# Sums of squares at the layer entries: wide VectorE additions for the second block, and modulation chunks, a value tile and DMAs at other places

## The chip, the core and the metric

The kernel runs on one core of a Trainium2 chip. The metric is the device time of one execution in microseconds, lower is better. Engines are named as in the profile: PE is TensorE, DVE is VectorE, ACT is ScalarE, POOL is GpSimd, SP is SyncE, which here issues the loads of the weights.

## The reference, cut to what matters

Two blocks run one after the other on x of 256 tokens by 1024 features, each with two layers. Block 1 is a mixer of two attentions and a convolutional feed-forward part, with norms that are scaled and shifted by a modulation `c @ mod_w`. Block 2 has five branches, one of them attention over a memory. Between the blocks stands the final norm of block 1.

```python
def _rmsnorm(x, g):
    xf = x.astype(jnp.float32)
    y = xf * lax.rsqrt(jnp.mean(xf * xf, axis=-1, keepdims=True) + EPS)
    return (y * g.astype(jnp.float32)).astype(x.dtype)

def first_block(...):
    for l in range(DEPTH):
        mod = c @ mod_w[l] + mod_b[l]
        sh1, sc1, g1, sh2, sc2, g2 = [m[:, None, :] for m in jnp.split(mod, 6, axis=-1)]
        h = _rmsnorm(x, norm1_g[l]) * (1.0 + sc1) + sh1
        x = x + g1 * _mixer(h, positions, w_in[l], ...)
        h = _rmsnorm(x, norm2_g[l]) * (1.0 + sc2) + sh2
        x = x + g2 * _conv_ffn(h, w_up[l], conv_w[l], conv_b[l], w_down[l])
    return _rmsnorm(x, final_g)

def second_block(x, mem, norm_pre, norm_post, ...):
    for l in range(DEPTH):
        h = rmsnorm(x, norm_pre[l])
        (...) = split_cols(h @ w_in[l])
        ...
        mem_kv = rmsnorm(mem, mem_norm[l]) @ w_mem_kv[l]
        ...
        x = x + rmsnorm(merged @ w_out[l], norm_post[l])
    return x
```

## The kernel before

**Layout.** Features lie on the partitions: x is eight tiles (KD = 8) of 128 features by 256 tokens. A weight matrix comes from memory in chunks of 1 MB, each of two blocks of 128x1024, into a ring of five buffers (`ring`). To keep float32 accuracy at PE's faster rate each block is split into a rounded part `w_hi` (ACT, L1649) and the rest `w_lo` (DVE, L2042); the input is split likewise into `h_hi` and `h_lo`, and PE does three matmuls for a product (L1351, L1352, L1357; L1389, L1390, L1395 for tiles with tokens on the partitions). Six split blocks are held (SPLIT), so a new block's `w_hi` must wait until PE has read the block six before it.

**The plan.** `plan()` writes one list of steps, and each engine goes through it and does its own part of each step. The order of the list is thus the order on every engine. Ahead of its part of a step ACT splits blocks up to `st.upto`, DVE up to `st.behind`, both set by which blocks PE has used so far (`st.first`). In the last two tiles of a row of statistics and at a root of block 2 the splits of DVE stand at other places than elsewhere (the end of DVE's loop).

**A norm.** Eight steps `stat` make the squares of x on ACT (L1683) into `h_val`. The step `root` sums them over the features by matmuls with ones into `sums`: either POOL has added tiles 0 to 4 and PE sums five tiles' sum and tiles 5 to 7 (L1413, L1416 three times), or, where x comes as a row of its own (`in_row`: the first norm in block 2's layers, with x just written by the final norm or by the sum of the branches), PE sums all eight (L1416 eight times). ACT then does Ln and Exp (L1688, L1690), DVE a Newton step (L2150 to L2156), and the step `norm` makes `h_val` on DVE (L2182), `h_hi` on ACT (L1746 with a shift, L1748 without), `h_lo` on DVE. PE's next tiles need h.

**What PE does while a norm is made.** In block 1 chunks of the modulation (step `mod`, eight matmuls of 32x256, L1435) fill the gap: `gap_mod` puts one ahead of the norm and one behind it, if the last row of four chunks has been taken up; `some_mod` puts the others between other tiles, 46 in all. In block 2 it is the keys and values of the memory, which need no h of x: at the first entry (layer 0, at 880 us) one tile of keys and two token tiles of values (`mv`), then the root; at the second entry (layer 1, at 1205 us) two tiles of keys, then the root, then the two token tiles of values.

**The SP queue** (L1304 to L1314) issues the loads of all 266 chunks in the order of their use, each when its ring buffer is free, and at the end stores x in two parts of four tiles.

Of the kernel before, what the change touches and what calls it, by code (L numbers as in the profile page):

```python
# [84 lines left out]
class Step:  # L85
# [8 lines left out]
    def __init__(self, kind, subs, first, l=None, t=None, j=None, i=None, k=None, n=None, v=None, W=None,  # L94
# [5 lines left out]
                 last_ready=None, group=None, early=None):  # L100
# [8 lines left out]
        self.gate, self.sc_taken, self.last_ready, self.group, self.early = gate, sc_taken, last_ready, group, early  # L109
# [70 lines left out]
def plan():  # L180
# [9 lines left out]
    state = dict(parts=[], summed=None, loaded=None, added={}, all_by_pe={})  # L190
# [84 lines left out]
    def stats(after, src, tiles=None):  # L275


        i = p.count("norm")
        in_row = bool(after) and isinstance(after[0], tuple)
        state["all_by_pe"][i] = in_row  # L280
        state["added"][i] = n = p.counts.get("added", 0) if in_row else p.count("added")
        for k in range(KD + 1):
            if tiles and k < KD:
                after.append(tiles(k))
            if k:
                p.add("stat", k=k - 1, i=i, n=None if in_row else n, atts=p.counts.get("att", 0), src=src, hn=p.counts.get("h_norm", 0),
                      after=after[k - 1] if after else None)
        return i

    def root(i, mode):  # L290

        p.add("root", i=i, n=None if state["all_by_pe"][i] else state["added"][i], atts=p.counts.get("att", 0), mode=mode)

    def gap_mod():
        if queue and not state["summed"]:
            mod(*queue.pop(0))

    def norm(kind, after, src, i=None, rooted=False, mods=False, **more):

        if i is None:  # L300
            i = stats(after, src)
        if not rooted:
            root(i, kind)
        if mods:
            gap_mod()
        hn = p.count("h_norm") if kind in ("mod", "gain", "mem") else None
        p.add("norm", mode=kind, i=i, hn=hn, src=src, **more)
        if mods:
            gap_mod()
# [32 lines left out]
    for l in range(L1):  # L342
# [151 lines left out]
        def down(j):  # L494

            if j < len(early):
                return early[j]
            ps = fm("dn", dn[j], j=j, l=l).ps
            some_mod()
            return ps  # L500
        x_stats = stats([], "x", down)
        reduce_mod()
    plan2(p, fm, plain, norm, stats, att, att_out, att_turn, x_stats)
# [5 lines left out]
def plan2(p, fm, plain, norm, stats, att, att_out, att_turn, x_stats):  # L509
# [20 lines left out]
    kv_taken[0] += token_tiles(v0, 2, what="mv", l=0, src="mem")  # L530
    p.add("load_bias", l=0, after=None)
    norm("gain", None, "x", first, l=0)
# [427 lines left out]
def program(nc, weights, small, const, levels, buckets, far, x_t, mem_t, pos, scratch, mod_rows, mem_root, out):  # L960
    p = schedule()
    ctx = ExitStack()
    with ctx:
# [147 lines left out]
        sums_ready = sem("sums_ready")  # L1111
        mean_ready = sem("mean_ready")
# [181 lines left out]
        def _(sp):  # L1294
# [18 lines left out]
            sp.wait_ge(stored, 16 * KD // 4)  # L1313
# [3 lines left out]
        def _(pe):  # L1317
# [86 lines left out]
            def root(st):  # L1404
# [622 lines left out]
        def _(ve):  # L2027
# [130 lines left out]

            def vals(st):
# [501 lines left out]
            do = dict(setup_tables=setup_tables, setup=setup, bias=bias, vals=vals, mod=mod, modred=modred, modsum=modsum, root=root, norm=norm, mem_again=mem_again,  # L2661
# [92 lines left out]
```

## Time and profile before

| | |
|---|---|
| Median of 3 runs | 1542.07 us (1542.05 to 1544.58) |
| Profiled execution: its own time | 1542.8 us |
| Profiled execution: span, first to last instruction | 1541.0 us |
| PE, PEld busy | 1496.3 us (97%), 1433.5 us (93%) |
| DVE, ACT, POOL busy | 1143.7 (74%), 833.4 (54%), 31.4 us (2%) |
| Mean granted clock of PE | 0.993 |
| Loads of the ring | 266 of 1,024 KB |

How to read it: busy time is that of the engine's own instructions; PE and PEld (its weight loads) overlap, and the ends of pipelined matmuls are modelled, so a matmul that is shown as 0.28 us long may begin 0.12 us after the one ahead. In the timelines the number in brackets is the time for which the engine stood idle ahead of the row, and what ended it. A count beside a matmul that stands alone in its row can hold its weight load too (eight matmuls and eight loads are "x16"). PEclk is the granted clock, 1.00 for 2.4 GHz and 0.50 for 1.2 GHz. "First entry" is block 2's layer 0, at 875 to 900 us, "second entry" its layer 1, at 1203 to 1226 us.

### The profile page before, as it was taken

The page shows a single profiled execution, that of the slowest core. Times are in us where ns is not written, and L with a number is a line of the kernel's source. Part 1 is how long each engine was busy: PE and PEld are TensorE (multiplying, and loading weights), DVE is VectorE, ACT ScalarE, POOL GpSimd, SP SyncE. Part 2 cuts the span into 40 slices and gives each one's busy share as a digit, 9 for nine tenths or more (in the row PEclk, how much of TensorE's full clock was granted, in tenths as well). Part 3 has the DMA queues.
Part 4 walks back from the last instruction along what each step waited for, and adds up shares of the span by engine and source line. Part 5 has one row for each costly group of instructions (what it writes and reads, how often), then busy time and mean ns, then how long its engine had stood idle before and what let it go on. Part 6 is the DMA issues. An engine that isn't in the chain of part 4 may idle for free.

```text
span 1541.0 us, 31309 instructions
## 1 busy us (share of the span) xinstructions
PE 1496.3 (97%) x12608; PEld 1433.5 (93%) x12608; DVE 1143.7 (74%) x2202; ACT 833.4 (54%) x1509; POOL 31.4 (2%) x36
## 2 busy tenths in 40 slices
PE   6999999999999999999999999999999999999997
PEld 4898898999998999989999989999999999999997
DVE  5758566888646586769996678878966988888774
ACT  3655545655435646446555655645555754645453
POOL 0000001000000000010001000000000000000000
PEclk9999999999999999999999999999999999999998
DMA  9654555676776452454545543443446444444430
GB/s 393 251 216 184 202 223 192 219 275 247 275 272 252 168 214 87 157 196 165 179 179 194 219 164 113 169 185 138 154 152 246 150 154 163 167 163 141 169 129 28
DMA packets 47840, 290.51 MB, mean 189 GB/s; under 512 B 9992, under 2 KB 12296, under 8 KB 13136
## 3 DMA queue, kind: packets, MB, share of 16 engines
q1 hardware_dynamic: 38880, 280.83, 49.0%
q10 hardware_dynamic: 8816, 7.67, 1.5%
q8 instruction: 101, 1.65, 0.4%
q14 instruction: 43, 0.35, 0.1%
HBM read 286.09 MB, written 2.39 MB: 187 GB/s over the span
## 4 chain that ended last, share of the span: by engine, by line
PE 57%; DVE 1%; ACT 1%; DMA 0%; issue 0%; DVEq 0%; ACTq 0%
PE bank L1351 17%; PE bank L1357 16%; PE bank L1352 16%; PE bank L1601 2%; PE sums L1526 1%; PE sums L1416 1%; PE bank L1390 1%; PE bank L1395 1%; PE bank L1389 1%; PE bank L1508 1%; PE bank L1499 1%; DMA mem_x<-mem_t 0%; DVE w_lo L2042 0%; ACT w_hi L1649 0%; PE bank L1533 0%
## 5 line engine op out<-in xcount | busy, mean ns | idle before, releaser
L1351 PE MATMUL bank<-h_hi,w_hi 128*128 128x256 f32 x2256 | 632.8, 288 | 8.9 <-ACT h_hi L1746 3.7
L1352 PE MATMUL bank<-h_hi,w_lo 128*128 128x256 f32 x2256 | 622.3, 283 | 0.0
L2042 DVE TENSOR_TENSOR w_lo<-ring,w_hi 128x1024 fp32r<-128x1024 f32 x436 | 523.4, 1222 | 106.4 <-ACT w_hi L1649 103.8
L1357 PE MATMUL bank<-h_lo,w_hi 128*128 128x256 f32 x2256 | 575.9, 283 | 0.0
L1649 ACT ACTIVATE w_hi<-ring 128x1024 fp32r<-128x1024 f32 x436 | 449.2, 1054 | 131.4 <-PE bank L1357 130.9
L1351 PEld LDWEIGHTS bank<-h_hi,w_hi 128*128 128x128 f32 x2256 | 432.8, 192 | 22.9 <-issue 17.9
L1352 PEld LDWEIGHTS bank<-h_hi,w_lo 128*128 128x128 f32 x2256 | 433.0, 192 | 0.6 <-issue 0.5
L1357 PEld LDWEIGHTS bank<-h_lo,w_hi 128*128 128x128 f32 x2256 | 405.2, 192 | 0.0
L1351 PE MATMUL bank<-a_hi,w_hi 128*128 128x256 f32 x352 | 99.6, 283 | 1.0 <-DVE w_lo L2042 0.7
L1352 PE MATMUL bank<-a_hi,w_lo 128*128 128x256 f32 x352 | 98.3, 279 | 0.0
L1357 PE MATMUL bank<-a_lo,w_hi 128*128 128x256 f32 x352 | 98.2, 279 | 0.0
L1389 PE MATMUL bank<-w_hi,h_hi 128*128 128x256 f32 (+1 forms) x304 | 86.6, 289 | 3.9 <-ACT h_hi L1746 2.9
L1390 PE MATMUL bank<-w_lo,h_hi 128*128 128x256 f32 (+1 forms) x304 | 85.7, 286 | 0.0
L1883 ACT ACTIVATE conv_a<-bank,sm 128x256 f32<-128x256 f32 x44 | 24.8, 564 | 105.2 <-PE bank L1357 105.2
L1395 PE MATMUL bank<-w_hi,h_lo 128*128 128x256 f32 (+1 forms) x304 | 81.7, 287 | 0.0
L1351 PE MATMUL bank<-y_hi,w_hi 128*128 128x256 f32 x288 | 79.3, 280 | 0.0
L1352 PE MATMUL bank<-y_hi,w_lo 128*128 128x256 f32 x288 | 78.8, 278 | 0.0
L1357 PE MATMUL bank<-y_lo,w_hi 128*128 128x256 f32 x288 | 75.7, 281 | 0.0
L1944 ACT ACTIVATE sig<-bank 128x256 f32<-128x256 f32 x80 | 30.3, 379 | 78.1 <-PE bank L1357 77.5
L1351 PEld LDWEIGHTS bank<-a_hi,w_hi 128*128 128x128 f32 x352 | 66.1, 188 | 4.7 <-issue 3.3
L1389 PEld LDWEIGHTS bank<-w_hi,h_hi 128*128 128x128 f32 x304 | 59.6, 196 | 7.2 <-issue 5.9
L1352 PEld LDWEIGHTS bank<-a_hi,w_lo 128*128 128x128 f32 x352 | 66.2, 188 | 0.0
(336 smaller groups left out, 2345.7 us busy)
## 6 DMA issues: line engine op xcount, KB each, us to landing
ring<-weights SPq DMA_DIRECT2D x266, 1024.0 KB, 4.9
pos_bias<-scratch ACTq DMA_DIRECT2D x4, 512.0 KB, 5.6
x<-x_t ACTq DMA_DIRECT2D x1, 1024.0 KB, 6.9
scratch<-line ACTq DMA_DIRECT2D x1, 1024.0 KB, 5.6
mem_x<-mem_t ACTq DMA_DIRECT2D x1, 1024.0 KB, 6.7
mem_second<-mem_t ACTq DMA_DIRECT2D x1, 1024.0 KB, 6.2
out_t<-x SPq DMA_DIRECT2D x2, 512.0 KB, 2.6
co<-const SPq DMA_DIRECT2D x1, 462.0 KB, 7.2
```

Source lines behind the costliest of these rows:

```text
L1351: pe.matmul(to, WH[:, b % SPLIT, o, :], hi[:, k, :], start=(i == 0), stop=False)
L1352: pe.matmul(to, WL[:, b % SPLIT, o, :], hi[:, k, :], start=False, stop=False)
L1357: last = pe.matmul(to, WH[:, b % SPLIT, o, :], lo[:, k, :], start=False, stop=(i == n - 1))
L1389: pe.matmul(o, q, WH[:, s:s + m.n, k, :], start=(k == 0), stop=False)
L1390: pe.matmul(o, q, WL[:, s:s + m.n, k, :], start=False, stop=False)
L1395: last = pe.matmul(o, q, WH[:, s:s + m.n, k, :], start=False, stop=(k == KD - 1))
L1416: m = pe.matmul(sums[:, 0:S], ones, hb[:, k, :], start=(st.n is None and k == 0), stop=(k == KD - 1))
L1601: m = pe.matmul(to[:, (2 * g + s) * P:(2 * g + s + 1) * P], k[half, g, s * P:s * P + P], q[half, g, t * P:t * P + P], start=True, stop=True)
L1649: act.activation(WH[:, b % SPLIT], ring_half(b), ACT.Copy).then_inc(w_hi, 1)
L1883: act.activation(to[:, st.j % 3, :], bank[u.bank][:, 0:S], ACT.Identity, scale=ss(("conv_w", st.l, 2), c), bias=ss(("conv_b", st.l), c)).t ...
L1944: act.activation(sig2[:, st.j % 4, :], bank[st.ps.bank][:, 0:S], ACT.Tanh, scale=0.5).then_inc(taken[st.ps.bank], 1)
L2042: ve.tensor_tensor(WL[:, b % SPLIT], ring_half(b), WH[:, b % SPLIT].bitcast(F32), ALU.subtract).then_inc(w_lo_v, 1)
```

## The change

Six edits are made together.

1. In the two norms that PE summed alone, DVE adds the squares: tiles 2, 3 onto 0, 1 once tile 3 is squared; tiles 6, 7 onto 4, 5 once tile 7 is; then these onto the first two. Each is one addition of 128x512. PE sums the two tiles that are left.
2. `norm` calls `gap_mod` twice ahead of the norm.
3. Behind the last tile of the down projection no chunk of the modulation stands any more.
4. At the first entry the root stands between the two token tiles of values.
5. SP waits for the chunk (0, 0, 3), the last of the first two rows of the modulation, to land before it issues the next load.
6. x is stored in four parts of two tiles.

```diff
@@ stats, root
+        row = p.count("added_row") if in_row else None
+        state["row"][i] = row
...
@@ norm
         if mods:
+            gap_mod()
             gap_mod()
@@ down
             ps = fm("dn", dn[j], j=j, l=l).ps
-            some_mod()
+            if j < KD - 1:
+                some_mod()
@@ plan2
-    kv_taken[0] += token_tiles(v0, 2, what="mv", l=0, src="mem")
+    values = token_tiles(v0, 2, what="mv", l=0, src="mem")
+    kv_taken[0].append(next(values))
     p.add("load_bias", l=0, after=None)
-    norm("gain", None, "x", first, l=0)
+    root(first, "gain")
+    kv_taken[0] += values
+    norm("gain", None, "x", first, rooted=True, l=0)
@@ block.sync
                 sp.dma_start(ring[c % RING][:], weights[c]).then_inc(loaded[c % RING], 16)
-            for k in range(0, KD, 4):
-                sp.wait_ge(x_z, (L2 - 1) * KD + k + 4)
-                sp.dma_start(out[:, k:k + 4], x[:, k:k + 4]).then_inc(stored, 16)
+                if kind == "mod" and what == (0, 0, 3):
+                    wait_loaded(sp, c)
+            for k in range(0, KD, 2):
+                sp.wait_ge(x_z, (L2 - 1) * KD + k + 2)
+                sp.dma_start(out[:, k:k + 2], x[:, k:k + 2]).then_inc(stored, 16)
...
@@ root of the tensor engine
-                for k in range(0 if st.n is None else ADDED + 1, KD):
-                    pe.wait_ge(sq_done, KD * st.i + k + 1)
-                    m = pe.matmul(sums[:, 0:S], ones, hb[:, k, :], start=(st.n is None and k == 0), stop=(k == KD - 1))
+                if st.row is not None:
+                    pe.wait_ge(row_sum, 3 * st.row + 3)
+                for k in range(2) if st.row is not None else range(ADDED + 1, KD):
+                    if st.row is None:
+                        pe.wait_ge(sq_done, KD * st.i + k + 1)
+                    m = pe.matmul(sums[:, 0:S], ones, hb[:, k, :], start=(st.n is None and k == 0),
+                                  stop=(k == (KD - 1 if st.row is None else 1)))
@@ vector engine
+            def stat(st):
+
+                if st.row is None or st.k not in (3, KD - 1):
+                    return
+                ve.wait_ge(sq_done, st.i * KD + st.k + 1)
+                a = st.k - 3
+                tt(hb[:, a:a + 2, :], hb[:, a:a + 2, :], hb[:, a + 2:a + 4, :], ALU.add).then_inc(row_sum, 1)
+                if a:
+                    ve.wait_ge(row_sum, 3 * st.row + 2)
+                    tt(hb[:, 0:2, :], hb[:, 0:2, :], hb[:, 4:6, :], ALU.add).then_inc(row_sum, 1)
```

DVE at the second entry, before: from the last sums of x (macc holds the normed sum of the branches) to the Newton step on `sums`.

```order
L2047 TENSOR_TENSOR macc_121<-macc_121,rsq 128x256
L2047 TENSOR_TENSOR x<-x,macc_121 128x256 x3
L2042 TENSOR_TENSOR w_lo<-ring4,w_hi 128x1024 x2
L2150 TENSOR_SCALAR mean2<-sums 128x256
L2047 TENSOR_TENSOR rsq<-guess 128x256
```

And now. `h_val_50<-h_val_50 128x512` is a wide addition of squares; the second and third wait for the last square and for each other.

```order
L2061 TENSOR_TENSOR macc_121<-macc_121,rsq 128x256
L2061 TENSOR_TENSOR x<-x,macc_121 128x256 x3
L2056 TENSOR_TENSOR w_lo<-ring4,w_hi 128x1024
L2061 TENSOR_TENSOR h_val_50<-h_val_50 128x512
L2056 TENSOR_TENSOR w_lo<-ring4,w_hi 128x1024
L2061 TENSOR_TENSOR h_val_50<-h_val_50 128x512 x2
L2164 TENSOR_SCALAR mean2<-sums 128x256
L2061 TENSOR_TENSOR rsq<-guess 128x256
```

The two splits stand where they stood, one on either side of the first addition, and the other two additions behind both. On PE the root's matmuls, now two, stand at their old place, between the keys and the values.

ACT at the first entry, before: the squares, the copies of the memory's keys and values (`mk_t`, `m_v`), the splits, the root and h.

```order
L1683 ACTIVATE h_val_50<-x 128x256 x8
L1914 ACTIVATE mk_t_96<-bank4 128x256
L1649 ACTIVATE w_hi<-ring1 128x1024
L1760 ACTIVATE m_v_97<-bank5 128x256
L1760 ACTIVATE m_v_97<-bank6 128x256
L1649 ACTIVATE w_hi<-ring2 128x1024 x2
L1907 DMA pos_bias_105<-scratch 128x4x256 x2
L1688 ACTIVATE guess<-sums,co 128x256
L1690 ACTIVATE guess<-guess 128x256
L1748 ACTIVATE h_hi<-h_val_50 128x256 x8
```

And now (lines are 14 further down in this function).

```order
L1697 ACTIVATE h_val_50<-x 128x256 x8
L1928 ACTIVATE mk_t_96<-bank4 128x256
L1663 ACTIVATE w_hi<-ring1 128x1024
L1774 ACTIVATE m_v_97<-bank5 128x256
L1921 DMA pos_bias_105<-scratch 128x4x256 x2
L1702 ACTIVATE guess<-sums,co 128x256
L1704 ACTIVATE guess<-guess 128x256
L1774 ACTIVATE m_v_97<-bank6 128x256
L1663 ACTIVATE w_hi<-ring2 128x1024 x2
L1762 ACTIVATE h_hi<-h_val_50 128x256 x8
```

The copy of the second value tile and two splits moved from ahead of the root to between the root and h.

The modulation's chunks on PE move by one place in the gaps of block 1: at 251 us three stand behind the sums (two before), at 465 us three behind them (one ahead and two behind before), at 676 us one (two before). Their number, 46, is the same.

## Rows read from the trace of the kernel before

**Rows 1.** Who waited for whom, of PE: total us, times, longest us.
```profile
PE bank L1351 <- ACT h_hi L1746: 3.7, 2, 1.9
PE bank L1351 <- ACT h_hi L1748: 3.6, 1, 3.6
PE bank L1389 <- ACT h_hi L1746: 2.9, 2, 2.0
```

**Rows 2.** Timeline of PE, first entry: start us, us, engine, line, tiles, count [idle].
```profile
884.22 0.28 PE L1389 MATMUL bank<-w_hi,h_hi 128*128 128x256 f32 x1
887.10 3.62 PE L1416 MATMUL sums<-h_val,co 128*128 128x256 f32 x16
894.35 0.36 PE L1351 MATMUL bank<-h_hi,w_hi 128*128 128x256 f32 x1 [3.63 <-ACT h_hi L1748]
```

**Rows 3.** Busy us by stretch: from:to, length, PE, PEld, DVE, ACT, POOL, PEclk, DMA.
```profile
680.00:684.00 4.00, 3.57 (x30) 3.60 (x31) 3.82 (x11) 2.60 (x6) 0.00 (x0) 1.00 1.01 428
895.00:898.00 3.00, 3.00 (x16) 3.00 (x15) 3.00 (x9) 1.74 (x5) 0.00 (x0) 0.50 0.03 5
474.00:478.00 4.00, 3.95 (x22) 3.98 (x23) 4.00 (x11) 2.35 (x5) 0.00 (x0) 0.64 1.02 428
```

**Rows 4.** Timeline of PE, second entry.
```profile
1210.71 4.28 PE L1416 MATMUL sums<-h_val,co 128*128 128x256 f32 x16
1214.63 0.47 PE L1389 MATMUL bank<-w_hi,mem_second_hi 128*128 128x256 f32 x1
```

**Rows 5.** Timeline of ACT, second entry.
```profile
1212.95 1.09 ACT L1683 ACTIVATE h_val<-x 128x256 f32<-128x256 f32 x3 [0.25 <-DVE x L2047]
1216.37 0.48 ACT L1688 ACTIVATE guess<-sums,co 128x256 f32<-128x256 f32 x1
```

**Rows 6.** Timeline of DVE, second entry.
```profile
1212.50 1.09 DVE L2047 TENSOR_TENSOR x<-x,macc 128x256 f32<-128x256 f32 x3
1213.51 2.36 DVE L2042 TENSOR_TENSOR w_lo<-ring,w_hi 128x1024 fp32r<-128x1024 f32 x2
```

**Rows 7.** Timeline of DVE: additions of 128x512 elsewhere.
```profile
1010.01 1.28 DVE L2047 TENSOR_TENSOR hg_exp<-hg_cum 128x512 f32<-128x512 f32 x2
```

**Rows 8.** Timeline of DVE, first entry.
```profile
884.26 1.21 DVE L2042 TENSOR_TENSOR w_lo<-ring,w_hi 128x1024 fp32r<-128x1024 f32 x1
```

**Rows 9.** Timeline of ACT, first entry.
```profile
887.30 0.38 ACT L1760 ACTIVATE m_v<-bank 128x256 f32<-128x256 f32 x1 [1.02 <-PE bank L1395]
888.53 1.05 ACT L1649 ACTIVATE w_hi<-ring 128x1024 fp32r<-128x1024 f32 x1
893.68 0.81 ACT L1748 ACTIVATE h_hi<-h_val 128x256 fp32r<-128x256 f32 x2 [2.00 <-DVE h_val L2182]
```

**Rows 10.** Timeline of PE, two gaps of block 1.
```profile
251.22 1.93 PE L1435 MATMUL bank<-ring,c_wide 128*32 128x256 f32 x32
...
676.64 1.93 PE L1435 MATMUL bank<-ring,c_wide 128*32 128x256 f32 x32
```

**Rows 11.** Timeline of DVE, gap at 465 us.
```profile
465.83 4.62 DVE L2042 TENSOR_TENSOR w_lo<-ring,w_hi 128x1024 fp32r<-128x1024 f32 x4
```

**Rows 12.** Line L1309, window 468 to 469: ring loads issued, and their landing.
```profile
L1309 SPq DMA_DIRECT2D ring<-weights x1: 328/328/328, 468.3 to 468.3; - x1
DMA to landing us min/median/max: 4.6/4.6/4.6
```

**Rows 13.** Line L1309, window 22 to 27.
```profile
L1309 SPq DMA_DIRECT2D ring<-weights x2: 327/328/328, 23.2 to 26.2; - x2
DMA to landing us min/median/max: 7.6/7.7/7.9
```

**Rows 14.** Timeline of PE and ACT, the start.
```profile
30.91 1.56 PE L1435 MATMUL bank<-ring,c_wide 128*32 128x256 f32 x16 [0.95 <-DMA ring<-weights]
37.78 3.89 ACT L1649 ACTIVATE w_hi<-ring 128x1024 fp32r<-128x1024 f32 x4
```

**Rows 15.** DMA issues: out<-in, queue, count, KB each, us to landing.
```profile
out_t<-x SPq DMA_DIRECT2D x2, 512.0 KB, 2.6
```

More of the change, by code:

```diff
@@ L99, in __init__ @@
                  lag=None, dir=None, prevn=None, k0=None, k1=None, ys=None, gate=None, sc_taken=None,
-                 last_ready=None, group=None, early=None):
+                 last_ready=None, group=None, early=None, row=None):
         self.kind, self.subs, self.first, self.upto, self.behind = kind, subs, first, None, None
@@ L108, in __init__ @@
         self.scale, self.lag, self.dir, self.prevn, self.k0, self.k1, self.ys = scale, lag, dir, prevn, k0, k1, ys
-        self.gate, self.sc_taken, self.last_ready, self.group, self.early = gate, sc_taken, last_ready, group, early
+        self.gate, self.sc_taken, self.last_ready, self.group, self.early, self.row = gate, sc_taken, last_ready, group, early, row
 class Plan:
@@ L188, in plain @@
         return p.matrix([tile_cols(name, lead, [(c0 + P * j, P)], rows) for j in range(n)])
-    state = dict(parts=[], summed=None, loaded=None, added={}, all_by_pe={})
+    state = dict(parts=[], summed=None, loaded=None, added={}, all_by_pe={}, row={})
     def mod(l, g, part):
@@ L285, in stats @@
             if k:
-                p.add("stat", k=k - 1, i=i, n=None if in_row else n, atts=p.counts.get("att", 0), src=src, hn=p.counts.get("h_norm", 0),
+                p.add("stat", k=k - 1, i=i, n=None if in_row else n, row=row, atts=p.counts.get("att", 0), src=src, hn=p.counts.get("h_norm", 0),
                       after=after[k - 1] if after else None)
@@ L290, in root @@
     def root(i, mode):
-        p.add("root", i=i, n=None if state["all_by_pe"][i] else state["added"][i], atts=p.counts.get("att", 0), mode=mode)
+        p.add("root", i=i, n=None if state["all_by_pe"][i] else state["added"][i], row=state["row"][i], atts=p.counts.get("att", 0), mode=mode)
     def gap_mod():
@@ L502, in plan, with plan2 @@
         reduce_mod()
-    plan2(p, fm, plain, norm, stats, att, att_out, att_turn, x_stats)
+    plan2(p, fm, plain, norm, root, stats, att, att_out, att_turn, x_stats)
     return p
-def plan2(p, fm, plain, norm, stats, att, att_out, att_turn, x_stats):
+def plan2(p, fm, plain, norm, root, stats, att, att_out, att_turn, x_stats):
     order = ("sc", "at", "mem", "cf", "hg")
@@ L1111, in program @@
         sums_ready = sem("sums_ready")
+        row_sum = sem("squares_of_a_row_added")
         mean_ready = sem("mean_ready")
@@ L1309, in _ @@
                 sp.dma_start(ring[c % RING][:], weights[c]).then_inc(loaded[c % RING], 16)
-            for k in range(0, KD, 4):
-                sp.wait_ge(x_z, (L2 - 1) * KD + k + 4)
-                sp.dma_start(out[:, k:k + 4], x[:, k:k + 4]).then_inc(stored, 16)
-            sp.wait_ge(stored, 16 * KD // 4)
+                if kind == "mod" and what == (0, 0, 3):
[3 more added lines that the diff above has]
+                sp.dma_start(out[:, k:k + 2], x[:, k:k + 2]).then_inc(stored, 16)
+            sp.wait_ge(stored, 16 * KD // 2)
         @block.tensor
@@ L2659, in m2end @@
                 m2_low(st.l, KD - 1)
-            do = dict(setup_tables=setup_tables, setup=setup, bias=bias, vals=vals, mod=mod, modred=modred, modsum=modsum, root=root, norm=norm, mem_again=mem_again,
+            do = dict(setup_tables=setup_tables, setup=setup, bias=bias, vals=vals, mod=mod, modred=modred, modsum=modsum, stat=stat, root=root, norm=norm, mem_again=mem_again,
                       rope=rope, decay=decay,
```

## Prediction

> **What bounds the kernel now.** I read the page first, then who waited for PE, then the timelines of the places that the change touches, then the granted clock by stretch. The page's first part shows PE busy for 97% of the span: what shortens PE's own row of work, or a wait of PE, shortens the run, and little else does. PE's waits are few and sit at the layer entries, where a sum of squares must pass through ACT and DVE before the next input h exists [rows 1]: 3.7 us for two gaps of block 1 that end on L1351 (at 255 and 680 us), 2.0 of the 2.9 for the gap at 474 us, 3.6 us at the first entry of block 2. There PE ends its work at 884.22 plus one token tile, 887.10, sums eight tiles of squares until 890.72, and then stands until 894.35 [rows 2]. That wait has a second price. After it the granted clock of 895 to 898 us is 0.50, the 1.2 GHz level, with 16 matmuls in 3 us, where 24 took 2.88 us from 884.22 to 887.10; it is 1.00, the 2.4 GHz level, from 680 to 684 us, after a wait of 1.9 us, and 0.64 from 474 to 478 us, after a shorter wait and one of 2.0 us with short chunks between [rows 3]. Three us at the lower level cost 1.5 us of PE.
>
> At the second entry of block 2, 1210 us, PE has no such wait: its eight sums begin at 1210.71, each as its square comes, and the value tiles begin at 1214.63 [rows 4]. The last three squares end at 1214.04, and ACT, busy with other work, takes the sum up only at 1216.37 [rows 5].
>
> **The second entry, PE's loss.** This is the largest term. PE's row now stands at one wait for three wide additions, with two sums behind it and 48 matmuls of the value tiles behind these. The additions stand on DVE among the splits of weights (w_lo). In the rows of before, x is finished at 1213.59, and two splits run from 1213.51 to 1215.87, so 1.18 us each, back to back with no wait [rows 6]. A wide addition of 128x512 is 0.69 us long, and two of them begin 0.59 to 0.6 apart (1.28 less 0.69) [rows 7]. In the new order: split until 1214.69; first addition (its squares are long done) until 1215.3; second split until 1216.5; second addition until 1217.1; the third waits for it, 0.1, and ends at 1217.8, 3.8 us after the last square. PE then does two sums. At the price of the first entry's eight, 3.62 / 8 = 0.45 us [rows 2], they end at 1218.7. Before, the value tiles began at 1214.63, so PE loses 4.1 us. ACT's Ln moves from 1216.37 to 1218.8, h is ready in time for the tile behind the value tiles, and nothing gives the loss back: PE has no wait behind it that could shrink.
>
> The same wait lasts from 1210.71 to 1217.8, 7.1 us, twice the one of 3.6 us that was followed by the lower clock. I take 4 us at 0.50 after it, 2.0 us of loss, between 0 (the clock spared) and 3.5 us (7 us of it, as long as at the first entry and again as much, as the wait is twice as long). Sum of this entry: 6.1 us, from 4.1 to 7.6. In case the splits did not stand in the way, the additions would end at 1214.1 + 0.6 + 0.1 + 0.6 = 1215.4 and the sums at 1216.3, which is 1.7 us instead of 4.1.
>
> The Trainium skill (TensorE: Matmul & The Clock Gate, section on how the gate's oscillation bites in real kernels) says that waits between groups of matmuls let the gate fall back to half rate, so that each group behind a wait starts slow. By it the 7.1 us are certain to cost clock, and both of the new waits at the first entry are suspect; the rows agree for 3.6 us and show that 1.9 us went free [rows 1 and 3].
>
> **The first entry.** Here the root now stands behind the first of two value tiles, so PE reaches it at 884.22. DVE ends x at 884.34 and would start its split at 884.26 [rows 8]; now the first addition comes first, until 884.9, the split until 886.1, then two additions, until 887.4. PE waits 3.2 us, sums two tiles until 888.4 (2.3 us sooner than 890.72), and does the second value tile, 2.88 us, until 891.3. The chain through ACT and DVE would give h at 888.4 + 3.63 = 892.0. But on ACT the copy of that second value tile and two splits (w_hi) now stand ahead of h_hi, and these splits overwrite the blocks that this tile reads. Before, from the end of this tile, 887.10, to the end of the splits, 889.58, is 2.5 us, and from the start of h_hi to PE's resumption 0.67 [rows 2 and 9]. So h_hi starts at 891.3 + 2.5 = 893.8 and PE resumes at 894.4 or 894.5, against 894.35: the 2.3 us are taken by the copy and splits, net 0.1, which I count as nothing. One wait of 3.6 us has become two, of 3.2 and of 3.1, around 3.8 us of work. If the clock falls in the first, the second value tile runs at half rate, up to 2.9 us more, and the next group as before: bounds are 1.6 us below nothing (no fall at all: 3.2 us at 0.50 are no longer there) and 4 us. I take 1.5, near the half of a tile, because 3.2 us is nearer to the wait that cost clock than to the one that did not. DVE's own two later splits move behind its norm as well; the blocks that they fill are read only after three more tiles, some 9 us, so I count 0 (2.4 us, two splits, if that cover failed).
>
> **The gaps of block 1.** A chunk of the modulation is 0.96 us of PE (two are 1.93 [rows 10]). The number of chunks is unchanged; what counts is how many stand in a wait. At 251 us there are three instead of two and the wait of 1.9 shrinks to 0.9: a gain of 0.96. At 465 us the one that stood ahead of the sums now stands behind them, so three as before. At 676 us there is one instead of two, since the other was used up earlier, and the wait grows to 2.8: a loss of 0.96 in the place where this chunk now runs. Net 0. Two things hang on it. At 465 us the third chunk needs a ring buffer that is free only when the second of four splits ends, 465.83 + 2.3 = 468.15 [rows 11]; a load issued at 468.3 there landed 4.6 us later, 472.9 [rows 12]. PE would have done two chunks by 471.3, waits until 472.9, and ends the third at 473.9, just ahead of h at 474.05: 0, up to 1 us. And DVE does four splits until 470.45 there and sums the modulation behind them before it looks at the root, so sums of squares that end sooner bring nothing. At 676 us a wait of 2.8 us may now bring the lower clock; 3.2 us of it cost 1.6. I take half, 0.8. That the fall at 474 us vanishes is the other bound, 1.5 us below nothing; its waits keep their lengths, so I take 0.
>
> **The start.** The queue now holds back the loads behind the last chunk of the first row. The loads issued at 23.2 and 26.2 us took 7.6 and 7.9 us [rows 13]: the first landed at 30.8, the second at 34.1, so one did not come at the expense of the other, the first was not slowed by more than the chunks ahead of it, and holding the second back speeds nothing. PE's wait for it is 0.95 us [rows 14], which bounds the gain. The later loads start up to 4.7 us later; the first is split by ACT at 37.78 [rows 14], and with 4.6 us to landing it comes at 35.5, 2.3 us ahead. I take 0, from 0.95 of gain to 1 of loss.
>
> **The end.** The store of 512 KB took 2.6 us to land [rows 15]. The last one is now 256 KB. At the rate of the load of 1,024 KB in 4.6 us [rows 12], the bound above is 256 / 1024 of 4.6, 1.2 us, the bound below nothing; I take 0.6.
>
> **The sum.** 6.1 + 1.5 + 0 + 0.8 + 0 - 0.6 = 7.8 us longer. The profiled execution took 1542.8 us with a span of 1541.0; its sum would be 1550.6. The median of the runs is 1542.07, and the forecast against it 1549.9 us, 0.5% slower.
>
> **The rivals.** First, the clock is spared (ends as no change): the two shorter waits of the first entry leave it at full (-1.6), so does the gap that ends at 474 us (-1.5), and the second entry pays only its 4.1, with the end's -0.6: +0.4, 1542.5 us. It is one mechanism, the clock's answer to a wait, and it decides from the wait of 7.1 us at 1210 us on. For it speaks that 1.9 us went free; against it, that 3.6 did not. Chance 0.12, for anything at or near this. Second, the clock answers worse: 4 at the first entry, 7.6 at the second, 1.6 at 676 us, 1 at 465, less 0.6: +13.6, 1555.7 us. For it speaks that the first entry has two waits in place of one; chance 0.13. Third, the wide additions are not held by the splits at the second entry, because DVE reaches them sooner than the rows of before allow: 1.7, with 1.5 of clock for a wait of 4.7 us, and the other terms as above (1.5 + 0.8 - 0.6): +4.9, 1547.0 us; against it stands the order, where one split is written between them; chance 0.15. My forecast has 0.55. The 0.05 left are for a real gain, for which no mechanism here adds up to 3 us.
>
> **From this to the numbers.** Faster or slower by over 0.2%, 3.1 us, is what a measurement of this kernel can tell from no change. Faster 0.05; same 0.15 (the first rival, a little of the third); slower 0.80. The range reaches from 1544.5, between the first and third rivals, to 1555.0, just short of the second.
>
> **What would show it.** At the second entry PE stands idle for some 7 us ahead of two sums, released by DVE's additions, with two w_lo ahead of them; a clock of 0.50 follows. At the first entry PE resumes with h within 0.5 us of the time after x that it has now, behind w_hi and not behind DVE. The gap at 676 us shows 2.8 us of wait. Wrong it would be if the second entry's sums are released under 2 us after the last square, or if the clock stays at 1.00 there.

## The result, and the profile after

The changed kernel took 1552.36 us (median of 4 runs, 1551.5 to 1553.35) against 1542.06 us for the kernel before in the same session (4 runs, 1541.78 to 1544.58): a ratio of 1.0060, 95% interval 1.0048 to 1.0072. It is 0.6% slower. The forecast was 1549.9 us, with a range from 1544.5 to 1555.0 and a chance of 0.80 for slower. The profiled execution took 1551.5 us, with a span of 1549.7.

PE's waits in the changed kernel, in the columns of [rows 1]:

```profile
PE bank L1449 <- DMA ring<-weights: 18.5, 4, 10.6
PE sums L1429 <- DVE h_val L2061: 10.2, 2, 7.0
PE bank L1361 <- ACT h_hi L1760: 3.7, 2, 2.7
PE bank L1361 <- ACT h_hi L1762: 2.9, 1, 2.9
```

The second row is new: PE waits for DVE's additions, 3.2 us at the first entry and 7.0 at the second. The wait for h_hi at the first entry has shrunk from 3.6 to 2.9 us, the one at 680 us has grown from 1.9 to 2.7.

**The second entry.** The timelines of PE, DVE and ACT answer to [rows 4 to 6]:

```profile
1220.72 2.05 PE L1429 MATMUL sums<-h_val,co 128*128 128x256 f32 x4 [7.01 <-DVE h_val L2061]
1222.20 0.78 PE L1399 MATMUL bank<-w_hi,mem_second_hi 128*128 128x256 f32 x1
...
1216.28 1.22 DVE L2056 TENSOR_TENSOR w_lo<-ring,w_hi 128x1024 fp32r<-128x1024 f32 x1
1217.42 0.69 DVE L2061 TENSOR_TENSOR h_val<-h_val 128x512 f32<-128x512 f32 x1
1218.02 1.22 DVE L2056 TENSOR_TENSOR w_lo<-ring,w_hi 128x1024 fp32r<-128x1024 f32 x1
1219.15 1.42 DVE L2061 TENSOR_TENSOR h_val<-h_val 128x512 f32<-128x512 f32 x2
...
1215.73 1.09 ACT L1697 ACTIVATE h_val<-x 128x256 f32<-128x256 f32 x3 [0.25 <-DVE x L2061]
```

The squares are done at 1216.82; DVE has two splits among its additions and ends them at 1220.57, 3.75 us later. PE's two sums then take 1.5 us in place of 0.9, because the clock has fallen; the value tiles begin at 1222.20, 16.1 us behind the mark at 1206.13 (the start of the root's matmuls on `mean`, shown below), where before they began 11.3 us behind it. Of these 4.8 us the lower clock inside the sums makes 0.6.

**The first entry** answers to [rows 2, 8 and 9]:

```profile
888.88 1.10 PE L1429 MATMUL sums<-h_val,co 128*128 128x256 f32 x4 [3.17 <-DVE h_val L2061]
897.21 0.55 PE L1361 MATMUL bank<-h_hi,w_hi 128*128 128x256 f32 x1 [2.87 <-ACT h_hi L1762]
...
892.42 0.88 DVE L2207 SCALAR_TENSOR_TENSOR h_val<-x,sm,rsq 128x256 f32<-128x256 f32 x2
...
894.38 0.38 ACT L1774 ACTIVATE m_v<-bank 128x256 f32<-128x256 f32 x1 [3.44 <-PE bank L1405]
894.66 1.99 ACT L1663 ACTIVATE w_hi<-ring 128x1024 fp32r<-128x1024 f32 x2
896.55 0.71 ACT L1762 ACTIVATE h_hi<-h_val 128x256 fp32r<-128x256 f32 x2
```

DVE has the first two tiles of h_val at 893.3, but ACT takes them up only at 896.55, behind the copy of the second value tile and two splits.

**The clock**, to be held against [rows 3]: from:to, length, PE busy, PEclk, DMA share, GB/s.

```profile
474.00:478.00 4.00, 3.08 (x33) 1.00 1.00 424
682.00:686.00 4.00, 4.00 (x24) 0.62 0.63 260
889.00:893.00 4.00, 4.00 (x20) 0.61 0.46 157
1219.00:1223.00 4.00, 2.28 (x7) 0.50 0.63 221
```

The fall at 474 us is gone; one at 682 us, one at 889, and the one around 1219 us are new. The last begins inside the wait: from 1216 us on the rows add up to 3.4 us of clock not granted, of which 1.8 fall behind the wait's end at 1220.72, where they cost PE something.

**Where the 8.7 us of span came from.** The root's matmuls on POOL's sum (L1413, now L1423) mark eight points of PE's row. The distances between them show each place by itself. The last two, of before and of after:

```profile
1203.34 0.59 PE L1413 MATMUL sums<-mean,co 128*128 128x256 f32 x2
1528.14 0.59 PE L1413 MATMUL sums<-mean,co 128*128 128x256 f32 x2
```

```profile
1206.13 0.59 PE L1423 MATMUL sums<-mean,co 128*128 128x256 f32 x2
1536.48 0.59 PE L1423 MATMUL sums<-mean,co 128*128 128x256 f32 x2
```

The same for every profile of this study (us; each column is the distance between two such starts, the last one that from the last start to the end of the span):

| kernel | start, to 249 | gaps of block 1, 249 to 834 | 834 to 877 | first entry, 877 to 1203 | second entry, 1203 to 1528 | end |
|---|---|---|---|---|---|---|
| before | 248.91 | 584.72 | 43.11 | 326.60 | 324.80 | 12.86 |
| store_alone | 249.07 | 583.78 | 43.47 | 326.57 | 324.79 | 12.82 |
| hold_alone | 248.26 | 583.96 | 43.10 | 327.48 | 324.78 | 12.82 |
| mods_alone | 249.69 | 585.45 | 43.11 | 326.60 | 324.78 | 12.87 |
| first_adds_alone | 248.60 | 584.01 | 43.12 | 326.55 | 324.78 | 12.84 |
| first_adds_moved | 252.93 | 584.08 | 43.10 | 328.23 | 324.79 | 12.87 |
| second_adds_alone | 251.76 | 584.55 | 43.47 | 326.57 | 330.66 | 12.79 |
| second_between | 250.62 | 583.61 | 43.11 | 327.60 | 326.26 | 12.80 |
| h_before_splits | 249.20 | 584.32 | 43.10 | 322.28 | 324.81 | 12.79 |
| gaps_filled | 248.43 | 582.40 | 43.11 | 323.81 | 324.78 | 12.87 |
| after | 250.38 | 584.22 | 43.47 | 328.06 | 330.35 | 13.22 |
| filled_wait | 249.26 | 584.09 | 43.10 | 328.21 | 328.56 | 13.18 |
| splits_later | 250.02 | 584.52 | 43.47 | 325.66 | 328.37 | 13.26 |

How to read it: where eight kernels do the same thing at the second entry they agree within 0.03 us, so a difference there is the edit's. The start differs by over 4 us among kernels that do the same, and the first entry by 1.1 us, so single profiles say less there. After less before is 1.47 - 0.50 + 0.36 + 1.46 + 5.55 + 0.36 = 8.70 us. The 0.36 from 834 to 877 us is no part of the change: 43.47 stands in four of the thirteen profiles, with the edits and without them (store_alone, second_adds_alone), and 43.1 in the others.

### The profile page after: what moved, and what is told of

The parts are those of the page before. It is cut to its first block, busy times and chain, and to the rows that moved or that the text cites. A ratio compares the mean times of both kernels' runs of the same rounds, so it can differ in the third digit from the quotient of the medians.

```text
span 1549.7 us, 31270 instructions
## 1 busy us (share of the span) xinstructions
PE 1492.4 (96%) x12584; PEld 1432.0 (92%) x12584; DVE 1148.8 (74%) x2208; ACT 833.9 (54%) x1509; POOL 31.3 (2%) x36
## 4 chain that ended last, share of the span: by engine, by line
PE 56%; DVE 3%; ACT 2%; issue 0%; DVEq 0%; ACTq 0%
PE bank L1361 16%; PE bank L1367 16%; PE bank L1362 16%; PE bank L1615 2%; PE sums L1540 1%; PE bank L1400 1%; PE bank L1399 1%; PE bank L1405 1%; ACT w_hi L1663 1%; DVE w_lo L2056 1%; PE bank L1522 1%; PE bank L1513 1%; PE sums L1429 0%; DVE macc L2061 0%; DVE x L2061 0%
## 5 line engine op out<-in xcount | busy, mean ns | idle before, releaser
L1449 PE MATMUL bank<-ring,c_wide 128*32 128x256 f32 x736 | 51.0, 401 | 18.5 <-DMA ring<-weights 18.5
```

The source lines that it names most:

```text
L1449: m = pe.matmul(to[q:q + 32, 0:256], cpad[:, k, :], w[:, k, :], start=(k < 4), stop=(k >= 4), tile_position=(0, q))
```

## The experiments

Each kernel was timed against runs of the kernel before on the same chip; these had medians of 1543.65, 1543.52 and 1543.33 us in the three sessions and scattered from 1539.8 to 1548.5, more than in the first one. So the ratios are the measure, and the table above shows where.

### The parts alone

**hold_alone**: before, and

```diff
                 sp.dma_start(ring[c % RING][:], weights[c]).then_inc(loaded[c % RING], 16)
+                if kind == "mod" and what == (0, 0, 3):
+                    wait_loaded(sp, c)
```

> The kernel before with one part of the change alone: the queue of loads waits for the last chunk of the first modulation row. By the prediction this costs nothing (0.95 us of gain to 1 us of loss): 1542.1 us. By a reading of the two profiles the held queue is what delays that chunk: in the changed kernel it is issued at 22.8 us and lands 8.9 us later, where before it took 7.6 to 7.9, PE waits 4.4 us for it and stands 1.5 us behind at 40 us. Then this kernel takes 1543.6 us, PE's wait ends near 31.7 us, and all the lag is there by 40 us. If the lag came from something else in the changed kernel, PE's first h is at 35.2 us as before.

Measured: ratio 1.0003 (0.9993 to 1.0012). PE's wait for the chunk and its first h, in this kernel:

```profile
30.36 1.07 PE L1445 MATMUL bank<-ring,c_wide 128*32 128x256 f32 x16 [0.64 <-DMA ring<-weights]
34.30 0.36 PE L1395 MATMUL bank<-w_hi,h_hi 128*128 128x256 f32 x1 [1.71 <-ACT h_hi L1756]
```

and in first_adds_moved, which holds nothing back at the start:

```profile
31.71 1.93 PE L1445 MATMUL bank<-ring,c_wide 128*32 128x256 f32 x16 [4.53 <-DMA ring<-weights]
```

My reading of the two profiles had been wrong: the late chunk is chance. From issue to landing it takes 7.5 or 7.6 us in nine of the thirteen profiles and 8.9 or 9.0 in four, two of these with the hold (after, splits_later) and two without (first_adds_moved, second_between). PE's first h comes between 34.3 and 36.5 us; the four with the hold have 34.30, 35.41, 36.32 and 36.45, the nine without it 34.76 to 36.39. The forecast value, 0, stands.

**mods_alone**: before, and

```diff
         if mods:
+            gap_mod()
             gap_mod()
...
-            some_mod()
+            if j < KD - 1:
+                some_mod()
```

> The kernel before with the moved modulation chunks alone: a second one in the gap before each norm of block 1, none behind the last down tile. The prediction had 0.8 us of loss (the wait of 2.8 us at 676 us brings the lower clock, 465 us is neutral): 1542.9 us. By the two profiles: 1.0 gained ahead of the sums at 465 us, 1.4 lost to the third chunk's load behind them, 1.5 gained since the clock does not fall at 474 us, 1.5 lost since it falls at 681 us, 0.7 to 0.9 gained at a wait for w_lo at 827 us if that wait vanishes. That is 0.5 us of gain at most: 1541.6 to 1542.3 us.

Measured: ratio 1.0009 (1.0000 to 1.0018), 0 to 2.8 us slower. PE at the gaps at 465 and 676 us, and the clock:

```profile
474.03 1.07 PE L1445 MATMUL bank<-ring,c_wide 128*32 128x256 f32 x16 [0.20 <-DMA ring<-weights]
681.44 0.55 PE L1357 MATMUL bank<-h_hi,w_hi 128*128 128x256 f32 x1 [2.72 <-ACT h_hi L1756]
```

```profile
682.00:686.00 4.00, 4.00 (x25) 0.66 0.73 307
```

The fall at 682 us stands in all four profiles with a wait of 2.7 us there, and in none of the eight with 1.9. It costs 1.5 us: from h to PE's next wait, for w_lo at 700 us, PE takes 19.1 us in all eight and 20.5 to 20.6 in the four. Earlier falls are another matter (below): over the whole stretch from 249 to 834 us the four kernels with the moved chunks have a mean of 584.57 us, the eight with the old ones 584.13, a loss of 0.4 us with a scatter as large. The forecast was 0.8. It is that small because three of the four have no other fall in this stretch, while each of the eight has one. In mods_alone, which has falls at 468 and 550 us besides, the third chunk at 465 us waits only 0.20 us for its load because the lower clock has made PE late (its two chunks ahead take 3.0 us in place of 1.9); in the other three it waits 1.8 to 2.0.

**first_adds_moved**: before, with edits 1 and 4 at the first entry only (`row` is counted only where `after[0][0] == "xn"`).

> The kernel before with the first entry of block 2 as changed (three wide additions, the root between the two value tiles), and nothing else. By the prediction: 0.1 us of logic, since h_hi on ACT stands behind the copy of the second value tile and two splits, and 1.4 of clock: +1.5 us, 1543.6 us, with a wait of 3.2 us ahead of the sums and one of about 3 behind the second value tile. By the rival in which the clock is spared it is 1.6 us of gain, 1540.5 us. The changed kernel's profile has PE's lag grow by 1.3 us there.

Measured: ratio 1.0007 (0.9995 to 1.0018). In the profile the first entry takes 328.23 us, 1.6 more than before's 326.60, and the changed kernel and filled_wait have 328.06 and 328.21. Both waits are there (3.2 and 2.9 us in its profile), and the clock falls behind both. The first fall slows the second value tile, so that h comes 19.1 us behind the mark, here and in the changed kernel (897.21 less 878.07), against 17.6 before. The clock:

```profile
892.00:896.00 4.00, 4.00 (x24) 0.57 0.14 46
899.00:903.00 4.00, 3.75 (x19) 0.57 0.02 4
```

The run's median shows 0.2 us, its interval reaches to 2.8, so the 1.5 us rest on the profiles: three with this code at 328.1 to 328.2, and seven with the code of before at the entry or with first_adds_alone's at 326.6 to 327.6.

**second_adds_alone**: before, with edit 1 at the second entry only.

> The kernel before with the three wide additions at block 2's second entry alone. By the prediction (two splits of weights stand among the additions, PE waits 7.1 us, then runs 4 us at the 1.2 GHz level) +6.1 us: 1548.2 us. By the rival in which the splits do not hold the additions it is 3.2 us: 1545.3 us. In the changed kernel's profile PE's lag grows by 5.6 us there; if that is the additions' own doing, the same must show here without the other parts: 1547.7 us.

Measured: ratio 1.0049 (1.0034 to 1.0064), 5.2 to 9.9 us; 1549.82 against 1543.65 us. The stage takes 330.66 us, 5.9 more than before. PE's wait and the clock:

```profile
PE sums L1423 <- DVE h_val L2055: 7.1, 1, 7.1
```

```profile
1218.00:1222.00 4.00, 1.07 (x3) 0.57 0.37 90
```

This one edit makes most of the result by itself, at the size forecast (6.1), and not at that of the third rival (3.2). The five ratios of the parts alone (the fifth, store_alone, follows) add up to 1.0064, against 1.0060 for all parts together, each known to 0.001 or 0.0015: no effect of the parts on each other is needed.

**store_alone**: before, with the four stores.

> The kernel before with its output stored in four pieces of 256 KB in place of two of 512 KB, and nothing else. The prediction had 0.6 us of gain (the last store lands sooner). In the profiles of the changed kernel and of two runs built on it, the time from the last value of x to the end is 3.1 us as before, and between mean and rsq on DVE 0.4 us of idle time stand that before has not. If the stores bring nothing and those 0.4 us come with another part, this kernel takes 1542.1 us and the last root to the end 12.8 us; if they come with the stores, 13.2 us.

Measured: ratio 0.9996 (0.9986 to 1.0005), end 12.82 us. The stores bring nothing: the 0.6 us of my sum were not there. I had scaled the time to landing with the size, and it hardly depends on it: 2.6 us for 512 KB [rows 15], and in this kernel

```profile
out_t<-x SPq DMA_DIRECT2D x4, 256.0 KB, 2.5
```

The 0.4 us of idle time on DVE that stand in the changed kernel's end come with none of the parts tried alone; they are in all three kernels that have all parts, and what makes them stays open (the rows are the changed kernel's).

```profile
1538.91 0.42 DVE L2164 TENSOR_SCALAR mean<-sums 128x256 f32<-128x256 f32 x1 [11.97 <-ACT guess L1702]
1539.78 0.43 DVE L2061 TENSOR_TENSOR rsq<-guess 128x256 f32<-128x256 f32 x1 [0.45 <-DVE mean L2164]
```

### What the second entry's loss is made of

**filled_wait**: the changed kernel, and ahead of PE's wait for the additions

```diff
+                for _ in range(14 if st.row == 1 else 0):
+                    pe.matmul(sums[:, 0:S], ones, one2, start=True, stop=True)
                 if st.row is not None:
                     pe.wait_ge(row_sum, 3 * st.row + 3)
```

> The changed kernel, and in PE's wait at block 2's second entry 14 more sums of constants, whose result is overwritten by the next one: work without use that keeps PE busy. 14 such sums at full clock take 6.3 us (0.45 each) of the wait of 7.0, and the additions end no sooner or later. By the prediction 2.0 of the entry's 6.1 us are the clock's answer to the wait: then the clock stays at 1.00 after it and PE's lag at 1235 us is 1.8 to 2.0 us less than in the changed kernel, 1550.5 us. By the rival in which all of the loss is the wait itself (the clock has nothing to do with it) the time stays, and the clock falls to 0.50 all the same.

Measured: ratio to before 1.0048 (1.0031 to 1.0065) against the changed kernel's 1.0060, intervals that overlap; the profile decides:

```profile
1212.03 6.21 PE L1425 MATMUL sums<-co 128*128 128x256 f32 x28
1219.16 1.13 PE L1431 MATMUL sums<-h_val,co 128*128 128x256 f32 x4 [0.93 <-DVE h_val L2063]
```

```profile
1219.00:1223.00 4.00, 3.84 (x29) 1.00 0.61 246
```

PE goes on at the same distance behind the mark (14.5 us against 14.6), the clock stays at 1.00, and the stage takes 328.56 us against 330.35. So 1.8 us of the 5.6 are the clock's answer to the wait (forecast 2.0) and 3.8 the wait and the sums (forecast 4.1; the value tiles begin at 1219.94, 4.0 us later against the mark than before).

**splits_later**: the changed kernel, on DVE

```diff
                 if st.kind == "norm" and st.mode in ("z", "gain"):
                     do[st.kind](st)
-                    split_to(st.behind)
+                    if st.mode == "gain":
+                        split_to(st.behind)
                     continue
-                if not root_next:
+                if not root_next and (st.kind != "stat" or st.row is None):
                     split_to(st.behind)
```

> The changed kernel, with the splits of weights on DVE (w_lo) written behind the three additions at both entries. By the prediction two splits of 1.18 us hold the additions at the second entry, one at the first: then PE's wait there is 7.0 - 2.3 = 4.7 us, released 1.5 us after the last square, and at the first entry 3.2 - 1.2 = 2.0 us. PE's lag falls by 2.3 us at the second entry, a little more if the clock is back sooner, and by 1.2 at the first: 1548.9 us against 1552.4. By the rival in which the additions wait for something else (the squares on ACT), the waits stay at 7.0 and 3.2 us.

Measured: ratio to before 1.0021 (1.0012 to 1.0030). The waits are 4.78 and 2.03 us, as forecast. At the second entry:

```profile
1215.99 2.04 PE L1429 MATMUL sums<-h_val,co 128*128 128x256 f32 x4 [4.78 <-DVE h_val L2061]
```

```profile
1216.00:1220.00 4.00, 4.00 (x15) 0.50 0.19 33
```

The second entry takes 328.37 us, 2.0 less than in the changed kernel. A wait of 4.8 us costs as much clock as one of 7.0 (2.1 us against 1.8, summed over the lowered stretch), so all of the gain is the wait itself. The first entry takes 325.66 us, 2.4 less: 1.2 by the split, and behind the wait of 2.0 us the clock did not fall.

**second_between**: before, with edit 1 at the second entry, the splits on DVE behind the additions, and

```diff
-            norm("gain", None, "x", first, l=l)
-            kv_taken[l] += token_tiles(v1, 2, what="mv", l=l, src="mem")
+            values = token_tiles(v1, 2, what="mv", l=l, src="mem")
+            kv_taken[l].append(next(values))
+            root(first, "gain")
+            kv_taken[l] += values
+            norm("gain", None, "x", first, rooted=True, l=l)
```

and ACT's splits of that norm behind its h_hi.

> The kernel before with the additions at the second entry alone, the splits behind them, and the root between the two value tiles, so that a tile covers them; on ACT two splits stand behind h_hi. PE: tile until 1213.6, wait until the additions end at 1215.5, sums until 1216.4, tile until 1219.3. DVE's two later splits end at 1217.9 and hold the root by 0.3 us; h comes 3.1 us behind that, at 1221.0, where before the second value tile ends at 1220.4. So 0.6 us slower, with two waits of 1.9 and 1.7 us that may cost 1.5 us of clock each: between +0.6 and +3.6 us, near +0.6 if waits under 2 us are spared. If what the additions cost at this entry (5.6 to 6.1 us) were no matter of cover, it would be +5 or more.

Measured: ratio 1.0008 (0.9999 to 1.0017). The stage takes 326.26 us, 1.5 more than before. Both waits are there at the forecast sizes or under:

```profile
1217.28 1.20 PE L1426 MATMUL sums<-h_val,co 128*128 128x256 f32 x4 [1.97 <-DVE h_val L2059]
1223.72 0.36 PE L1358 MATMUL bank<-h_hi,w_hi 128*128 128x256 f32 x1 [0.98 <-ACT h_hi L1759]
```

```profile
1218.00:1222.00 4.00, 4.00 (x22) 0.57 0.37 98
```

The fall of the clock behind the first wait slows the second value tile, and h_hi stands behind that tile's copy on ACT. The same fall at the first entry, in the same order, is worth 1.5 us (gaps_filled against h_before_splits), so without it this order would be level with before. That is an estimate; no profile of this kernel is without the fall. A value tile as cover takes away nearly all of the edit's own cost, and the additions win nothing here even then, because before PE had no wait at this place.

### What took the first entry's gain

**first_adds_alone**: before, with edit 1 at the first entry only; the root stays behind both value tiles.

> The kernel before with the three wide additions at the first entry alone; the root stays behind both value tiles. PE then does two sums from 887.4 to 888.4 us in place of eight until 890.7. If that shortened the chain to h by as much, h would come 2.3 us sooner. By what the prediction says of ACT, two splits (w_hi) stand ahead of Ln there and end at 889.6 us, and a third w_lo on DVE ends at 889.9: Ln starts at 889.6 instead of 890.76 and h comes 1.2 us sooner, at 893.2, behind a wait of 4.8 us in place of 3.6. Time 1540.9 us at a before of 1542.1, with one fall of the clock as before.

Measured: ratio 0.9993 (0.9984 to 1.0002). From the start of the sums on `mean` to h it takes 16.31 us (892.04 less 875.73) where before took 17.61 (894.35 less 876.74): h is 1.3 us sooner, as by the splits, and not 2.3. On ACT Ln stands right behind the two w_hi:

```profile
887.51 1.05 ACT L1657 ACTIVATE w_hi<-ring 128x1024 fp32r<-128x1024 f32 x1
888.45 0.47 ACT L1696 ACTIVATE guess<-sums,co 128x256 f32<-128x256 f32 x1
```

PE's wait is 4.4 us in place of 3.6 and the clock lost behind it is 2.9 us, against 1.7 in before: the stage takes 326.55 us, and nothing is won. (Hold_alone and second_between lose 2.7 and 2.9 there with the 3.6 us of before, so the longer wait needn't be why.)

**h_before_splits**: before, with edits 1 and 4 at the first entry, DVE's split behind the additions, and on ACT

```diff
+                late = late or st.kind == "norm" and st.mode == "gain"
                 if late:
                     do[st.kind](st)
                 split_to(st.upto)
```

> The kernel before with the first entry as changed, the split on DVE behind the additions, and two splits on ACT behind h_hi instead of ahead of it. PE: wait from 884.2 to 886.2 us, sums until 887.1, second value tile until 890.0; h at 887.1 + 3.6 = 890.7, held by the copy of the tile to 890.9, against 894.35 before: 3.5 us sooner, and 5 us if two waits of 2.0 and 0.9 us spare the clock that falls after 3.6. So 1536.9 to 1538.6 us at a before of 1542.1. If the copy and splits were not what took the additions' gain in the changed kernel, h stays within 0.5 us of where it was.

Measured: 1539.17 us against 1543.52, ratio 0.9970 (0.9960 to 0.9980). This kernel is faster than both. PE and ACT:

```profile
886.29 1.10 PE L1425 MATMUL sums<-h_val,co 128*128 128x256 f32 x4 [2.03 <-DVE h_val L2058]
891.24 0.36 PE L1357 MATMUL bank<-h_hi,w_hi 128*128 128x256 f32 x1 [0.98 <-ACT h_hi L1758]
...
890.30 0.38 ACT L1770 ACTIVATE m_v<-bank 128x256 f32<-128x256 f32 x1 [1.94 <-PE bank L1401]
890.58 0.71 ACT L1758 ACTIVATE h_hi<-h_val 128x256 fp32r<-128x256 f32 x2
```

```profile
888.00:892.00 4.00, 3.02 (x25) 1.00 0.27 93
892.00:896.00 4.00, 4.00 (x36) 1.00 0.01 4
```

h comes 14.62 us behind the mark where before took 17.61, 3.0 us sooner (3.5 forecast), and the clock stays up, so the stage takes 4.3 us less. The same additions and the same root, with three splits in other places, turn a loss of 1.5 us into a gain of 4.3. Of the gain 3.0 us are h and the rest the fall that didn't come; in gaps_filled, with the same order, a fall came and the entry's gain is 2.8 us (323.81).

**gaps_filled**: h_before_splits, and on PE

```diff
             def norm(st):
+                if st.mode == "mod" and st.i:
+                    pe.wait_ge(mean_ready, st.i + 1)
+                    for _ in range(3):
+                        pe.matmul(sums[:, 0:S], ones, one2, start=True, stop=True)
```

> The kernel of the run h_before_splits, and at the norms at 251, 465 and 676 us three more sums of constants on PE (1.4 us of the 1.9 to 2.0 of wait), whose result nobody reads. In ten profiles so far the clock fell once or twice between 100 and 600 us, behind one of the waits at 117, 255, 472 or 550 us, not always the same. If any wait of 1 to 2 us can bring the fall, a filled one can't: then none stands at 255 and 474 us, the waits at 117 and 550 us are as before, and the time is 0.8 us less than that of h_before_splits (half of 1.6), 0.9965 of the kernel before. If the fall has nothing to do with these waits it stands at 474 us in as many runs as before, and the time is the same, 0.9970.

Measured: ratio 0.9967 (0.9955 to 0.9980), not to be told from h_before_splits. The profile has no fall from 40 to 884 us (249 to 834: 582.40 us, the shortest of all), but one at the first entry, behind the wait of 2.0 us that was free in h_before_splits:

```profile
473.00:477.00 4.00, 4.00 (x41) 1.00 0.99 414
884.00:888.00 4.00, 4.00 (x20) 0.57 0.64 223
```

That doesn't show that the filled waits spared it: three of the four kernels with the moved chunks (after, filled_wait, splits_later) have no fall between 100 and 600 us either, with waits of 2.1 and 1.8 to 2.0 us at 470 us left as they are.

## Why the prediction was right, step by step

- **The second entry's wait** (+4.1 of logic): right in its mechanism and size. Forecast: DVE's additions 3.8 us behind the last square, a wait of 7.1. Found: 3.75 and 7.01. splits_later shows that the two splits are what holds the additions, filled_wait that 3.8 us are left without the clock.
- **Its clock** (+2.0, 4 us at half rate): 1.8 measured, 3.6 us at half rate behind the wait.
- **The first entry** (+1.5): right in the sum and in what holds h. After the additions h stands behind the second value tile's copy and two splits, and first_adds_moved alone shows 1.6. The division was off: I had one fall of the clock partly counted. There are two, of 1.7 and 1.4 us, against one of 1.7 before. And one sign that I had named failed: h was to come within 0.5 us of its old time after x, and it came 1.5 us later behind the mark (19.1 against 17.6), because the first fall slows the value tile that h waits for.
- **The gaps of block 1** (+0.8): the sum was about right (0.4, with as much scatter), and in part by luck. The fall behind the wait of 2.7 us came each time and cost a full 1.5 us, not half of it; the other fall in this stretch, which each of the eight profiles with the old order of chunks has, was absent in three of the four with the new one. I had named that as a bound (1.5 us) and counted 0. The load of the third chunk at 465 us was read rightly: in the changed kernel PE waits 1.98 us for it (1.6 by my times, 472.9 less 471.3), and its next tile begins 8.9 us after the last part of x, against 8.6 before, a loss of 0.3 us within the bound of 1.
- **The end** (-0.6): wrong, a term with nothing behind it: a store of 256 KB takes 2.5 us to land and one of 512 KB 2.6. And 0.4 us of idle time appear on DVE, unexplained.
- **The start** (0): right, though the changed kernel's own profile seemed to say 1.5.
- **The rivals.** The clock spared (1542.5): it fell at every place where the wait grew to 2.7 us or more. The clock worse (1555.7): it needed 4 us at the first entry and 7.6 at the second, where 1.5 and 5.6 were found. The splits not in the way (1547.0): refuted by the 7.01 us and by second_adds_alone; where splits_later takes them out of the way, the entry loses 3.6 us, near that rival's 3.2.

The forecast's sum was 7.8; from the stages shown it is 0 + 0.4 + 1.5 + 5.6 + 0.4 = 7.9 us. That the two agree within 0.1 us is luck: the end is 1.0 us worse than forecast, the gaps 0.4 and the second entry 0.5 better. The two medians differ by 10.3 us, and the interval is 7.4 to 11.1 us, which has the forecast near its lower end. The changed kernel's profile has 1.5 us more at the start, which is chance; whether the rest of the difference between the stages and the medians is chance too, these runs don't show.

## What to carry to other kernels

A cheaper sum is worth only what the queue behind it lets through: look, on each engine of the chain, at what stands written between the input's arrival and the next link, since work for later (here splits of weights, 1.0 to 1.2 us each) placed ahead of it becomes part of the wait. Where PE has cover that needs no result of the chain, put it inside the chain and put the other engines' later work behind it; where PE had no wait, as at the second entry here, moving work from PE to another engine made one and won nothing, in either order that was tried. And count a new wait of PE of 3 us at some 1.5 to 2 us more than its length, for the clock (1.4 to 2.9 us behind the waits of 2.7 to 7 us here).

## What the runs showed of the hardware that I had not expected

**The same wait brings the clock down in one execution and not in another.** Eight profiles have the old waits between 100 and 600 us (1.1 us at 117 and 550, 1.9 at 255, 2.0 at 472). Each shows one or two falls, and not at the same places: four at 474 to 478 us, two at 256 to 258, two at 550 to 552, two at 118 to 120. Each adds up to 1.7 us of clock not granted and costs 1.5 us of time: from h at 474 us to PE's wait at 550 us it takes 76.9 us in the four profiles with the fall and 75.4 in the other four. Two examples, second_adds_alone and hold_alone:

```profile
118.00:122.00 4.00, 3.73 (x21) 0.68 0.60 248
258.00:262.00 4.00, 4.00 (x25) 0.67 1.01 426
```

```profile
474.00:478.00 4.00, 4.00 (x35) 1.00 1.01 420
551.00:555.00 4.00, 4.00 (x25) 0.67 0.02 4
```

Behind a wait of 2.0 us at the entries it fell in second_between and gaps_filled and not in splits_later and h_before_splits. Waits of 2.7 us and more had a fall each time, behind them or begun inside them, at these places: 680 us, the first entry, the second. So one profile can't price a wait of 1 to 2 us. The Trainium skill (TensorE: Matmul & The Clock Gate, section "What you observe") says of a row of back-to-back matmuls that the moment at which the clock rises varies from run to run; here it is more than the moment, since the same wait has a fall in one execution and none in another.

This goes with part of the scatter among executions. Of the 73 runs of the kernel before in the three later sessions, the 20 with a mean granted clock of 0.991 or less took 1545.2 us on average, the 26 with 0.992 took 1543.6, and the 27 above it 1542.7.

**One load lands at one of two distances in time.** The chunk that PE waits for at 30 us is issued at 22.4 to 23.2 us and lands 7.5 to 7.6 us later in nine profiles and 8.9 to 9.0 in four, whether the queue is held or not. What decides between them isn't shown. PE's first h varies by 1.6 us among the nine kernels with the same first 30 us.
